# A table for the attention's batches, row sums on VectorE, and other orders for the first gathers, the old keys' copies and the entry

## What is computed

```python
# per query tile: three branches, each a softmax over its keys
logits = q @ k * SM_SCALE + bias            # per kv group g and head r
p = softmax(where(mask, logits, NEG))
o = p @ v
# merge of the branches: compressed, selected, window
g = sigmoid(gate)                           # per token, branch and head
o = g[0] * o_c + g[1] * o_s + g[2] * o_w
a_out = o * silu(z_a)
...
# samples: the keys and values of 8 samples, 4096 past tokens each, are gathered by a page table
```

## Time and profile before

| | before |
| --- | --- |
| median of 3 runs (lowest, highest) | 947.78 us (947.65, 950.33) |
| the profiled execution, its own time | 957.26 us |
| its span | 955.4 us |
| TensorE matmuls busy | 896.9 us, 94% |
| VectorE busy | 600.8 us, 63% |
| ScalarE busy | 371.0 us, 39% |
| GpSimd busy | 105.3 us, 11% |
| mean granted TensorE clock | 0.978 of full |

### The profile page before, as it was taken

One profiled execution on the slowest core, in us unless ns is written; L12 is line 12 of the kernel. 1 busy time (PEld: TensorE's weight loads), 2 busy tenths in 40 slices (PEclk: granted clock), 3 DMA queues, 4 the chain that ended last, 5 costly groups with the idle time before them and its releaser, 6 DMA issues.

```text
span 955.4 us, 16015 instructions
## 1 busy us (share of the span) xinstructions
PE 896.9 (94%) x6261; PEld 573.2 (60%) x6261; DVE 600.8 (63%) x1129; ACT 371.0 (39%) x844; POOL 105.3 (11%) x105
## 2 busy tenths in 40 slices
PE   6999999999999999997999999997885999999997
PEld 4656665666666666665667776775643666544443
DVE  4698879999789887976465666566632444322221
ACT  4312262110113001135887787766633656411111
POOL 0012100000010111101002202120240230000000
PEclk9999999999999999998999999999897999999999
DMA  8435542412144366542600000000135988532111
GB/s 298 162 132 179 196 154 58 60 59 67 44 139 161 110 208 206 207 202 61 235 2 2 2 2 2 2 2 2 45 135 240 353 301 328 213 122 88 70 52 55
DMA packets 32110, 118.34 MB, mean 124 GB/s; under 512 B 3433, under 2 KB 11771, under 8 KB 22971
## 3 DMA queue, kind: packets, MB, share of 16 engines
q0 software_dynamic: 9360, 68.16, 19.6%
q1 hardware_dynamic: 19053, 43.39, 12.9%
q10 hardware_dynamic: 3623, 5.76, 2.9%
HBM read 108.33 MB, written 13.29 MB: 127 GB/s over the span
## 4 chain that ended last, share of the span: by engine, by line
PE 76%; DVE 8%; DMA 7%; ACT 3%; DVEq 2%; issue 2%; POOL 1%; ACTq 0%; SPq 0%; POOLq 0%
PE PS L833 26%; PE PS L2038 12%; PE PS L1587 6%; PE PS L1577 6%; DMA main<-in_cmp_v_dram,row 5%; PE PS L1605 5%; PE PS L809 3%; PE PS L1889 3%; PE PS L1868 3%; PE PS L1900 2%; DVE main L606 2%; PE PS L1555 2%; PE PS L1923 2%; ACT main L1397 2%; DMA main<-in_sel_k_dram,row 2%
## 5 line engine op out<-in xcount | busy, mean ns | idle before, releaser
L833 PE MATMUL PS<-main 128*128 128x352 f32 (+1 forms) x1056 | 331.5, 473 | 0.0
L833 PEld LDWEIGHTS PS<-main 128*128 128x128 f32 x1056 | 202.2, 192 | 121.3 <-issue 4.4
L1397 ACT ACTIVATE main<-PS,main 128x512 f32<-128x512 f32 (+3 forms) x192 | 103.9, 562 | 43.3 <-DVE main L1426 21.0
L2038 PE MATMUL PS<-main 128*128 128x512 f32 x256 | 112.3, 593 | 0.1
L434 ACT ACTIVATE main<-PS 128x384 f32<-128x384 f32 x24 | 11.8, 491 | 210.2 <-PE PS L833 204.0
L644 DVE SCALAR_TENSOR_TENSOR main<-main,par 128x1022 f32<-128x1022 f32 (+16 forms) x66 | 83.9, 1271 | 5.3 <-issue 0.4
L603 DVE TENSOR_TENSOR main<-main 128x1024 f32<-128x1024 f32 x64 | 75.5, 1221 | 16.2 <-DMA main<-in_cmp_v_dram,row 10.4
L2038 PEld LDWEIGHTS PS<-main 128*128 128x128 f32 x256 | 47.6, 190 | 56.4 <-issue 56.4
L1587 PE MATMUL PS<-cst,main 128*128 128x128 f32 x528 | 73.5, 288 | 8.3 <-ACT main L1397 8.2
L606 DVE TENSOR_TENSOR main<-main 128x1024 f32<-128x1024 f32 (+2 forms) x96 | 75.0, 781 | 7.2
L1389 ACT ACTIVATE main<-PS 128x512 f32<-128x512 f32 (+1 forms) x138 | 69.7, 597 | 18.3 <-PE PS L1587 18.1
(11 more groups left out here) (317 smaller groups left out, 1029.5 us busy)
## 6 DMA issues: line engine op xcount, KB each, us to landing
main<-in_w_tiles_dram SPq DMA_DIRECT2D x24, 512.0 KB, 3.6
out_dram<-main SPq DMA_DIRECT2D x18, 256.0 KB, 2.1
main<-in_x_prompt_dram SPq DMA_DIRECT2D x8, 512.0 KB, 9.2
main<-in_w_out_dram SPq DMA_DIRECT2D x4, 1024.0 KB, 5.9
main<-in_x_prompt_dram SPq DMA_DIRECT2D x16, 256.0 KB, 2.9
out_dram<-main SPq DMA_DIRECT2D x4, 512.0 KB
diag<-in_win_k_dram SPq DMA_DIRECT2D x8, 256.0 KB, 7.3
diag<-in_win_v_dram SPq DMA_DIRECT2D x8, 256.0 KB, 7.3
```

The lines of the kernel that those rows point to most:

```text
L833: last = pe.matmul(bank(3 * s + j)[:, 0:w], ring[:, s, k * P:(k + 1) * P], xT[:, k, t0:t0 + w], start=(k == 0), stop=(k == KD - 1))
L1397: last = act.activation(prob[:, k % 2, g, h * nk_ * P:(h + 1) * nk_ * P], score_set(k, g)[:, h * nk_ * P:(h + 1) * nk_ * P], ACT.Exp, scal ...
L2038: last = pe.matmul(out_bank(m, h), proj[:, MIX[k], n * P:(n + 1) * P], wo[:, k, h * 512:(h + 1) * 512], start=(x == 0), stop=(x == KD - 1))
```

## The change

Nothing of the result changes. In the order of the program:

- the constants are loaded behind the first tile of x, no longer ahead of it;
- the copies of the samples' old window keys and values from input to output (2 x 2016 KB) are issued behind the 12 stores of `sp_natural`, no longer ahead of them;
- the scores of the first batch run ahead of the prompt turn, which goes to banks 4 to 7 and is copied by VectorE behind the first peaks;
- a table (`PLAN`) sets the batches: tiles 7, 0, 6, 1, 5, 4, 2, 3, and each four-headed step stands beside another step, mostly an ordinary one (7E beside 7W, 0K beside 7W, 0L and 6E beside 6F, 5E and 4E beside 5W, 4F beside 4N; 4N once alone). There are 35 batches again. Tiles 0, 1 and 2 get a third set of buffers;
- the exps of four-headed steps give no sum; VectorE sums them (`row_sums`), in two instructions a step;
- VectorE does the second peak of a batch behind the first slot's `part_out` and side, and the gaps of a finished tile in the same place;
- the sides move with the tiles: none is left for the decode, where three were before (0c, 0K, 0L);
- `pool_decode` issues each round's value gathers behind the key gathers, also in round 0.

```diff
         def sp_startup(sp):
-            sp.dma_start(cst[:, :], dram["constants"]).then_inc(ld_cst, 16)
             for n in range(3):
                 sp.dma_start(xn[:, n, :], dram["x_prompt"][n * P:(n + 1) * P, :]).then_inc(ld_x[n], 16)
+                if n == 0:
+                    sp.dma_start(cst[:, :], dram["constants"]).then_inc(ld_cst, 16)
...
         def sp_natural(sp):
-            for k, key in enumerate(("win_k", "win_v")):
-                sp.dma_start(outs[11 + 2 * k][0, :, 0:WIN - DS].rearrange("b w g d -> b w (g d)"), dram[key][:, DS:, :]).then_inc(out_done, 16)
             wait_natural(sp)
...
+            for k, key in enumerate(("win_k", "win_v")):
+                sp.dma_start(outs[11 + 2 * k][0, :, 0:WIN - DS].rearrange("b w g d -> b w (g d)"), dram[key][:, DS:, :]).then_inc(out_done, 16)
...
-                last = pe.transpose(bank(0, 4)[:, k * P:(k + 1) * P], sc[:, k * P:(k + 1) * P], ident)
+                last = pe.transpose(bank(4, 4)[:, k * P:(k + 1) * P], sc[:, k * P:(k + 1) * P], ident)
             last.then_inc(SEM["cmp_pt_ps"], 1)
 
-        def act_prompt_turn(act):
-            act.wait_ge(SEM["cmp_pt_ps"], 1)
+        def dve_prompt_turn(dve):
+            dve.wait_ge(SEM["cmp_pt_ps"], 1)
             flat = ptc.rearrange("p i g q -> p (i g q)")
             for h in range(2):
-                act.activation(flat[:, h * T:(h + 1) * T], bank(2 * h, 2), ACT.Copy)
-            act.drain().then_inc(SEM["cmp_pt"], 1)
+                dve.tensor_copy(flat[:, h * T:(h + 1) * T], bank(4 + 2 * h, 2))
+            dve.drain().then_inc(SEM["cmp_pt"], 1)
...
+        PLAN = """7F 7F, 7F 7F, 7N 7N, 7N 7N, 7W 7W, 7W 7E, 7W 0K,
+            6F 0L, 6F 6E, 6F 6F, 6N 6N, 6N 6N, 6W 6W, 6W 6W, 1K 1K, 1L 1L,
+            5F 5F, 5N 5N, 5N 5N, 5W 5W, 5W 5E, 5W 4E, 4N 4F, 4N 4N, 4N, 4W 4W, 4W 4W,
+            2K 2K, 2K 2K, 2L 2L, 2L 2L, 3K 3K, 3K 3K, 3L 3L, 3L 3L"""
...
+        SUMMED = [k for k in range(NS) if STEPS[k][7] == R]
...
             def exp(k):
                 i, c, br, k0, nk_, kind, r0, heads = STEPS[k]
+                if k - 2 in SUMMED:
+                    act.wait_ge(SEM["row_sum"], SUMMED.index(k - 2) + 1)
                 for g in range(G):
                     act.wait_ge(SEM["s_max"], 2 * k + g + 1)
+                    if k == 0 and g == 0:
+                        act.wait_ge(SEM["cmp_pt_ps"], 1)
                     for h in range(heads):
                         u = c * 8 + (r0 + h) * 2 + g
+                        if heads == R:
+                            last = act.activation(prob[:, k % 2, g, h * P:(h + 1) * P], score_set(k, g)[:, h * P:(h + 1) * P], ACT.Exp, scale=-1.0, bias=peaks_of(i)[:, u:u + 1])
+                            continue
                         last = act.activation(prob[:, k % 2, g, h * nk_ * P:(h + 1) * nk_ * P], score_set(k, g)[:, h * nk_ * P:(h + 1) * nk_ * P],
-                                              ACT.Exp, scale=-1.0, bias=peaks_p[:, i % 2, u:u + 1], accum_out=sums[:, i % 2, u:u + 1])
+                                              ACT.Exp, scale=-1.0, bias=peaks_of(i)[:, u:u + 1], accum_out=sums_of(i)[:, u:u + 1])
                     last.then_inc(SEM["p_sb"], 1)
...
+            def row_sums(k):
+                i, c, br, k0, nk_, kind, r0, heads = STEPS[k]
+                dve.wait_ge(SEM["p_sb"], 2 * k + 2)
+                for g in range(G):
+                    u = c * 8 + g
+                    last = dve.tensor_reduce(sums_of(i)[:, u:u + 2 * R - 1:2], prob[:, k % 2, g, :].rearrange("p (h n) -> p h n", h=R), X, ALU.add)
+                last.then_inc(SEM["row_sum"], 1)
+                dve.drain()
...
+            dve_prompt_turn(dve)
             for b in range(TAIL + 1):
-                for j, k in enumerate(batch(b - 1)):
-                    if k + 1 == PARTS[PART_OF[k]][3]:
-                        part_out(PART_OF[k])
-                        dve.drain()
-                    for m, item in enumerate(SIDE):
-                        if item[0] == (b, j):
-                            side(m)
+                for j in range(2):
+                    if j < len(batch(b - 1)):
+                        k = batch(b - 1)[j]
+                        if k == PARTS[PART_OF[k]][3]:
+                            part_out(PART_OF[k])
+                            dve.drain()
+                        for m, item in enumerate(SIDE):
+                            if item[0] == (b, j):
+                                side(m)
+                    if j == 0:
+
+                        for k in batch(b)[1:] if b > 0 else []:
+                            peak(k)
+                        for i in ORDER:
+                            if i >= 4 and done_batch(i) == b:
+                                dve.drain()
+                                gaps(i)
                 for m, item in enumerate(SIDE):
                     if item[0][0] == b == TAIL:
                         side(m)
+                for k in batch(b):
+                    if k in SUMMED:
+                        row_sums(k)
                 for i in ORDER:
                     if done_batch(i) == b:
                         weights(i)
-                for k in batch(b + 1):
+                for k in batch(b + 1)[:1]:
                     peak(k)
-                for i in ORDER:
-                    if i >= 4 and done_batch(i) - 1 == b:
-                        dve.drain()
-                        gaps(i)
...
-            pe.wait_ge(SEM["cmp_pt"], 1)
-            for h in range(2):
-                pe.wait_ge(taken[(M_VN + h) % 2], (M_VN + h) // 2 + 1)
-            pe.wait_ge(SEM["vb_ready"], 1)
...
+            natural_free(pe, 6)
+            natural_free(pe, 7)
             for k in BATCH[0]:
                 scores(k)
+            for h in range(2):
+                pe.wait_ge(taken[(M_VN + h) % 2], (M_VN + h) // 2 + 1)
+            pe_prompt_turn(pe)
+            pe.wait_ge(SEM["vb_ready"], 1)
+            pe.wait_ge(SEM["cmp_pt"], 1)
             for b in range(TAIL + 1):
...
         def pool_decode(pool):
             pool.wait_ge(SEM["oz"], NT)
             pool.wait_ge(SEM["nat_out"], 16 * N_NAT)
-            for h in range(2):
-                pool_values(pool, 0, h)
             for rnd in range(4):
                 for h in range(2):
                     if rnd < 3:
...
                         pool_keys(pool, rnd + 1, h)
                     if rnd >= 1:
                         pool.wait_ge(SEM["vused"], 2 * (rnd - 1) + h + 1)
-                        pool_values(pool, rnd, h)
+                    pool_values(pool, rnd, h)
 
         def sp_decode(sp):
```

116 lines of the change are left out of this document (61 added, 55 removed).

## The result

The changed kernel takes 940.86 us (median of 4 runs, 940.48 to 941.44), the kernel before 949.06 in the same rounds (947.65 to 951.02): a ratio of 0.9904, 95% interval 0.9883 to 0.9925: about 1% faster. I had forecast 925.6, and 916 to 937 as the range. The time lies above the range.

A forecast was written before the change was run, and what follows sets the result against it. TensorE, busy 94%, was taken as the bound, so time could come only from its gaps and slow clock. Terms -0.4 - 5.1 + 1.7 - 4.0 - 14.4 = -22.2 from 947.78 gave 925.6 us; range 916 to 937.

The forecast's parts named there:

- the part on the table: Pairs: new batch table, sums on VectorE and peaks between sides were to bring -4.0 us, bounds -14 and +5.
- Against 23.5: Pairs: 18 us of losses after, plus 0.9 for one more side, set against 23.5 lost before; -4.6, taken as -4.0.
- that walk: Pairs after the change, losses walked with single durations: 10.4 us in summed batches, the rest from delayed second peaks; together 18.
- (c): Rival: the pairs gain nothing or lose, VectorE holding ordinary peaks behind the sums; +4 for -4, 933.6 us; chance 0.14.
- (a): Rival: the gather ahead of the pairs stays late for a reason of its own; 928.3 us; chance 0.07.
- (b): Rival: the decode's first keys land late, sharing with the values behind them; 6.5 us less gain, 932.1; chance 0.12.
- (d): Rival: short stops beside the sums keep TensorE at 1.2 GHz through nine whole batches; +50 us, 975; chance 0.03.
- a sign of being wrong: Pairs: granted clock falling in the summed batches was to show the forecast wrong; no size given.
- (e): Rival: nothing moves, gathers in the decode's later rounds give the gain back; 947 to 948 us; chance 0.03.
- Copies and entry: Ahead of the pairs: constants -0.4 us; 7.6 gained by copies and entry, of which 5.1 survive the stores' wait.
- the fall of the clock: Entry: TensorE stands about 2.5 us for the stores, then one spell of low clock costs +1.7, bounds 0 and 3.4.
- The end: Decode: second round starts 22.3 us behind the pairs' last turns, before 37.1, with no wait for keys; -14.4 us kept.

The follow-up runs named there:

- peaks by sides: Changed kernel, but the second peak stands between the slots only in batches with two sides, else both behind sums and weights: 933.92 us, 0.9805 of before.
- second profile of before: The kernel before, unchanged, profiled once more: 951.44 us (1 run).
- second profile of the change: The changed kernel, unchanged, timed and profiled once more: 941.61 us, 0.9881 of the kernel before.

## Why the prediction was wrong

**The step that failed** is the last of the part on the table: "Against 23.5". I walked through the batches after and summed TensorE's waits, 18. For before I had no walk: I took the time of the pairs less the work in full batches of 5.71 and sides of 0.95. These are two different measures. What remained, 23.5, held TensorE's waits and all that is longer than a full batch's share of turns: turns of 16 in 3.62 us at the lower clock, scores of other shapes. The windows from b to E say how much of it was waits (us; busy of PE, PEld, DVE, ACT, POOL; PEclk, DMA share, GB/s). Before:

```profile
474.78:690.86 216.08, 200.90 (x2102) 150.64 (x2102) 138.30 (x324) 158.05 (x480) 36.87 (x29) 0.98 0.02 6
```

After:

```profile
467.26:689.40 222.14, 203.29 (x2093) 148.26 (x2093) 151.89 (x340) 151.72 (x422) 36.83 (x29) 0.99 0.03 11
```

The changed kernel with its peaks by sides:

```profile
467.08:682.26 215.18, 200.92 (x2093) 146.98 (x2093) 151.40 (x340) 151.92 (x423) 36.81 (x29) 1.00 0.04 13
```

TensorE stood 15.2 us before (216.08 - 200.90), not 23.5, and 18.9 after, where I had walked to 18. Waits against waits, the term is 18 + 0.9 - 15.2 = +3.7 and not -4.0. The measured +6.1 is 3.7 of waits and 2.4 of busy time: a side (0.9), and 1.5 for products that take longer, such as the mixed batches' (TensorE is busy 6.18 us in 7W 7E, 5.71 in a full batch) and those at the lower clock behind 6F 0L. With +3.7 the sum would have been -14.5 and the forecast 933.3. With its peaks by sides TensorE stands 14.3.

Read batch by batch, the waits show what the table did. Before, 3.8 us stand in the pairs 7E 6E and 5E 4E and in 4F, and 11.0 in tiles 2 to 0. After, 8.9 stand in the seven mixed batches, 3.3 in 1K and 1L, 4.7 in tile 2, 1.3 in the first 4W 4W, 0.4 at 3L. The stops of four-headed steps were not hidden behind an ordinary step, they were spread over more batches. Part of the agreement of 18 with 18.9 is luck: in tile 2 I counted only what the split adds, and at twice its size (4.0, it added 2.0), and left out waits that stood there before.

**The terms of that walk.** The seven mixed batches were to lose 10.4 over 5.86 and lose 11.9 (7.12, 7.12, 8.92, 7.68, 7.13, 7.11, 7.83, together 52.9; 12.9 over 5.71). The prices of single operations were close: two sums take 1.28 us (1.3), four exponentials without their read 1.14 (0.27 each). Of the split peaks I had priced the harm: 1.2 at the first 4W 4W, 4.0 in tile 2, 0.3 at 3L. Freed of it, the kernel gains 7.0 in the pairs, 1.7, 2.0 and 0.8 at these places, and 2.5 in the summed batches 6F 0L, 6F 6E and 4N 4F, where I had seen none. I saw a cost there and took it as given; it was the cheapest thing to mend.

**Slips in its sums.** The chain of 7W 7E adds up to 6.8, not 6.9; 5.86 for TensorE's share stands in no row (a full batch is 5.71); half of what the better bounds add gives 918 as the lower end, not 916. None bears on the step that failed.

**Rivals.** (c), the pairs lose, had the sign and two thirds of the size (+4, 933.6). Its mechanism, ordinary peaks held up by the sums, is refuted as the cause of the net loss: without VectorE's sums the pairs are 4.0 longer. (a) fell, the gather came in time. So did (b): the keys weren't waited for. (d) did not come at its size, the granted clock in the pairs is 0.99; but it did fall in one summed batch, 0.78 behind 6F 0L, which I had named as a sign of being wrong. (e) is refuted by the value gathers alone.

**Copies and entry.** Predicted -0.4 - 5.1 + 1.7 = -3.8 at b. ScalarE's first x comes at 4.68 instead of 5.11, 0.4 as said. Between the two profiles b moved by 7.5, but 3.8 of that was the first profile's accident ahead of 400 us; against the second profile of before it is 2.7 and 4.2, in the change's two profiles. At the scores behind the first turns, where I had 7.6, it is 6.2 (451.49 to 445.30). The single parts: copies -3.1, entry 0. The mechanism held in most links: what is gained ahead is lost again in the stores' wait (of the entry's 2.0 in its own run only half, the other half in slow scores), TensorE stands (3.14 us; I had 2.5), and the fall of the clock costs 3.18 + 2.37 - 2 x 1.97 = 1.6 for the 1.7 expected. In the second profile of the change it stood 2.46 and the clock did not fall for the values (1.97). And the rule of the Trainium skill (DMA: Bandwidth & Descriptors, section "Queues, rings and completion order"), that a DMA engine takes turns between the queue rows with work, does not excuse the copies: with them ahead the slowest gather took 28.2, 25.6, 25.4 and 17.0 us in four profiles, with them behind 12.6 at most in sixteen. How the engines shared out the packets no run shows; what failed is only my inference that such a gather would land long before the copies were through.

**The end.** Predicted -14.4, and the second round 22.3 behind E. Measured 23.0 (712.36 - 689.40), and the tail is 14.3 shorter than in the first profile, 13.4 than in the second; the change's second profile has 12.1 to 13.0. The parts: 8.1 by the gathers' order, 3.9 by the sides that left (254.1 to 250.2). This step was right, to 1 or 2 us.

**The base.** The time lies 15.3 us above the forecast, 1.3 of it because the kernel before took 949.06 in these rounds and not 947.78. Of the other 14.0 (22.2 against 8.2), 10.1 are the pairs and 1 to 2 are what the first profile of before had more than an ordinary execution at the two places that I priced from it (3.8 against 2.7 to 4.2 at b, 14.4 against 13.4 in the tail). The rest lies within what two timings differ by: repeated, the change brings 11.1 (952.71 to 941.61).

## What to carry to other kernels

Compare like with like: if the losses after are a sum of waits read or walked one by one, read the losses before in the same way, from TensorE's busy time in the same stretch, and not as time less ideal work. Where an in-order engine has an order that helps some batches and hurts others (here the second peak ahead of or behind a side), let each batch choose by what it holds: it brought 7.0 us in the pairs where neither fixed order did. And move what a next stage waits for (keys) ahead of what it wants later (values) in the issuing queue: two lines brought most of the change's gain.
